# A transformer stack in fp32 on one core: the opening in one stage, norm first and bias tables last

## The chip, the core and the metric

The kernel runs on one core of one Trainium2 chip. The metric is the device time of one execution in microseconds (us), as the median of several runs. The engines are named as the profile names them: PE is the matrix engine (TensorE), PEld its weight load, DVE is VectorE, ACT is ScalarE, POOL is GpSimd, SP is SyncE. SP and ACT also issue transfers (DMAs), each on a queue of its own: the profile calls SP's queue q1 and ACT's q10. Both feed the same 16 DMA engines.

## The reference, cut to what matters

The program computes a whole stack: first a dilated attention layer and a state space layer, then four layers of other kinds, each with a feed forward part. Sequence 512, width 1024, all in fp32. The change touches only what comes ahead of the first projections, and three tables of relative position bias that later layers read.

```python
h = rms_norm(x, attn_pre_norm[0])                 # x: (1, 512, 1024)
proj = h @ w_in                                   # w_in: 1024 x 10240
for g, (window, dilation) in enumerate(((128, 1), (512, 4), (2048, 16))):
    bias = rel_bias[t5_bucket(jnp.maximum(back, 0) * dilation)]      # table bias_a
    logits = einsum(q, k) * scale + bias
...
# layers 0 and 3 of the second part read a causal 512-wide table (bias_d),
# layer 2 a windowed 256-wide one (bias_s), both from rel_bias of that part
s = jnp.where(rel >= 0, s + bias, -jnp.inf)
```

## The kernel before, in words

**Weights.** All weights are one stream of 270 chunks of 128x2048 fp32 (1 MB each). SP loads chunk c into one of two `raw` buffers; POOL splits it into a high part `wh` and a low part `wl` (two instructions, two buffers of each); PE multiplies both with the split activations `XTh` and `XTl`, three matmuls for one product (`three`, lines 326 to 328). Three rules tie the stream together. `load_chunk` (line 290) issues the load of chunk c once chunk c-2 has been split (`w_split`). `split_chunk` (lines 296 and 298) begins on chunk c once it has landed and once PE has used chunk c-2 (`w_used`). PE waits for the split of chunk c at its first tile. Chunks are counted from 0.

**The opening.** It has two stages, each a block that all engines enter and leave together.
- `setup` (line 370 on): SP loads chunks 0 to 3 and POOL splits chunks 0 and 1. ACT issues the loads of two one-hot matrices (33 rows), of the small bias tables, of x and of four norm vectors. PE makes the three tables by four matmuls of one-hot by bias (line 436), DVE copies them out of PSUM to `ta` (16 heads x 893) and `tb` (16 x 1022). ACT then issues five transfers that write each row of a table 128 times to HBM, each time shifted by one element (`toeplitz`, line 423): three for `bias_a` (rows of 256, 128 and 128 elements), one for `bias_d` (16 heads x 128 rows x 512), one for `bias_s` (16 x 128 x 256). The profile's 2048 KB, 1024 KB and so on of line 423 are the sizes of these; together 10 MB. Then ACT leaves the block.
- `norm_phase("pre")`: ACT takes the squares of X (line 501), POOL turns the sums into factors (480, 481), DVE scales X by rows into `N` (546), PE transposes N (587), DVE multiplies by the norm weight, a column now (532), ACT copies the high part (515), DVE forms the low part (535). SP waits for `bias_a` to be in HBM before the block ends.

**The attention stage** (`dilated_attention`, one block). It uses chunks 0 to 39 in four passes of ten. Ahead of the passes PE makes the 18 tiles of chunks 0 to 5 without a break (four v tiles for chunk 0, two for chunk 1, four for 2, two for 3, four for 4, two for 5), through two PSUM banks that ACT empties in turn (`take`, lines 1338 to 1344). In the passes such tiles are filled in between the steps of eight attention jobs. ACT loads a pair of heads of `bias_a` to `B` (line 1387), first ahead of its first `take`, then once a half pass. SP runs the stream for chunks 4 on (`sp_stream`) and waits for all tables before it leaves the block.

```python
        def toeplitz(dst, table, off, w, sig=bias_a_stored):
            x = table[:, off:off + w]
            src = bass.AP(x.tensor, x.offset + P - 1, [list(x.ap[0]), [-1, P], [1, w]])
            act.dma_start(dst, src).then_inc(sig.h, 16)
```

Of the kernel before, what the change touches and what calls it, by code (L numbers as in the profile page):

```python
# [23 lines left out]
P = 128  # L24
S = 512
D = 1024
# [191 lines left out]
def build(nc, t, out):  # L218

    ctx = ExitStack()  # L220
    with ctx:
# [70 lines left out]
        def split_chunk(pool, c, r, s):  # L292
# [4 lines left out]
            pool.wait_ge(w_high.h, c + 1)  # L297
            pool.tensor_tensor(wl[s][:, :], raw[r][:, :], wh[s][:, :].bitcast(F32), ALU.subtract).then_inc(w_split.h, 1)  # L298

        def stream(eng, first, last, unit, one):  # L300
# [57 lines left out]
        x_back = signal("x_back")  # L358
        v_moved = signal("v_moved")
        bias_ds_stored = signal("bias_ds_stored")  # L360

        def wait_bias_stored(eng):
# [7 lines left out]
        def setup(a_scope, b_scope):  # L370

            with ExitStack() as c:
                tb = sb("tb", [HEADS, LB], F32, b_scope)
                ta = sb("ta", [HEADS, LA], F32, a_scope)
# [3 lines left out]
                made = signal("made")  # L378
                tables = signal("tables")
                with nc.Block() as block:  # L380
                    @block.sync
                    def _(sp):
                        for k in range(min(RAW, NCH)):
                            sp.dma_start(raw[k][:, :], t["weights"][k]).then_inc(raw_in[k].h, 16)
                        for k in range(RAW, min(RAW + SPLIT, NCH)):
                            load_chunk(sp, k, k % RAW)

                    @block.gpsimd
                    def _(pool):
                        link = InOrder(pool, pool_order)  # L390
                        link(pool.memset(zero[:, :], 0.0))
# [7 lines left out]
                        link.done()  # L399
                        for s in credited:  # L400
                            pool.sem_inc(s.h, CREDIT)
                        for k in range(min(SPLIT, NCH)):
                            pool.wait_ge(raw_in[k % RAW].h, 16 * (k // RAW + 1))
                            pool.tensor_tensor(wh[k][:, :], raw[k % RAW][:, :], zero[:, :].to_broadcast([P, CHUNK]), ALU.add).then_inc(w_high.h, 1)
                            pool.wait_ge(w_high.h, k + 1)
                            pool.tensor_tensor(wl[k][:, :], raw[k % RAW][:, :], wh[k][:, :].bitcast(F32), ALU.subtract).then_inc(w_split.h, 1)

                    @block.scalar
                    def _(act):
                        for d, s in ((oh_a[:, :], t["onehot_a"]), (oh_b[:, :], t["onehot_b"]),  # L410
                                     (rb[0:32, 0:HEADS], t["rel_bias"]), (rb[0:32, HEADS:], t["rel_bias_2"]),
                                     (X[:, :, :], t["x"].rearrange("b (t p) d -> p (b t) d", p=P)),
                                     (col[:, 0:KT], t["attn_pre_norm"]), (col[:, KT:2 * KT], t["ssm_pre_norm"]),
                                     (col[:, 16:18], t["da_subln_2"]), (col[:, 18:19], t["hg_gnorm_2"])):
                            act.dma_start(d, s).then_inc(loaded.h, 16)

                        act.wait_ge(tables.h, 4)

                        def toeplitz(dst, table, off, w, sig=bias_a_stored):

                            x = table[:, off:off + w]
                            src = bass.AP(x.tensor, x.offset + P - 1, [list(x.ap[0]), [-1, P], [1, w]])
                            act.dma_start(dst, src).then_inc(sig.h, 16)
                        toeplitz(bias_a[:, :, 0:W1], ta, 0, W1)
                        toeplitz(bias_a[:, :, W1:384], ta, L1, W2)
                        toeplitz(bias_a[:, :, 384:512], ta, L1 + L2, W2)
                        toeplitz(bias_d, tb, 0, WD, bias_ds_stored)
                        toeplitz(bias_s, tb, LD_, WS, bias_ds_stored)
                        act.wait_ge(loaded.h, 16 * 9)

                    @block.tensor
                    def _(pe):
                        pe.wait_ge(loaded.h, 16 * 9)
                        pe.wait_ge(made.h, 2)
                        for n, (o, lo, hi, r) in enumerate(((oh_a, 0, 512, 0), (oh_a, 512, LA, 0), (oh_b, 0, 512, 1), (oh_b, 512, LB, 1))):
                            nc.tensor.matmul(PS[n][0:HEADS, 0:hi - lo], rb[:, HEADS * r:HEADS * r + HEADS], o[:, lo:hi],
                                             start=True, stop=True).then_inc(p_b.h, 1)

                    @block.vector
                    def _(dve):  # L440
                        for n, (o, lo, hi) in enumerate(((ta, 0, 512), (ta, 512, LA), (tb, 0, 512), (tb, 512, LB))):
                            dve.wait_ge(p_b.h, n + 1)
                            nc.vector.tensor_copy(o[:, lo:hi], PS[n][0:HEADS, 0:hi - lo]).then_inc(tables.h, 1)
                loaded.base += 16 * 9
                p_b.base += 4

# [795 lines left out]

        sink_tmp = sb("sink_tmp", [P, 8])

        def dilated_attention():
            c0 = pos[0]
            with ExitStack() as c:
                O3 = sb("O3", [P, 3, 8, S], F32, c)  # L1250
# [2 lines left out]
                with ExitStack() as c2:  # L1253
# [98 lines left out]
                    with nc.Block() as block:  # L1352
                        @block.sync
                        def _(sp):
                            sp_stream(sp, 40)
                            wait_bias_stored(sp)

                        @block.gpsimd
                        def _(pool):
                            pool_stream(pool, 40)  # L1360

                        @block.tensor
                        def _(pe):
# [11 lines left out]
                                    att[half].pe(at, fill)  # L1375
                            for n in range(len(first)):
                                project(pe, 0, 0, 0, n)
                            with pe.Fori(0, PASSES - 1) as i:
                                one_pass(i, False)
                            one_pass(PASSES - 1, True)  # L1380
# [2 lines left out]
                        def _(act):  # L1383
# [5 lines left out]
                            def one_pass(i, last):  # L1389
                                for half in range(2):  # L1390
# [32 lines left out]
                        @block.vector  # L1423
                        def _(dve):
                            link = InOrder(dve, dve_order)
                            with dve.Fori(0, PASSES) as i:
                                link.enter(i, sum(x.dve_links() for x in att))
                                for half in range(2):
# [16 lines left out]
                    PROJ.base += 4 * n_proj  # L1445
                    BIAS_IN.base += 128
                    BIAS_USED.base += 8
                    pos[0] += 40
                combine_groups(O3, MX, SM)

# [1122 lines left out]


        with ExitStack() as b_scope:
            with ExitStack() as a_scope:
                setup(a_scope, b_scope)
                if "attn" in STAGES:
                    norm_phase("pre", gain=col[:, 0:KT], before_end=wait_bias_a_stored)
                else:  # L2580
                    norm_phase("plain", before_end=wait_bias_stored)
            if "attn" in STAGES:
                dilated_attention()
        if "attn" in STAGES:
            out_phase(None, (t["attn_post_norm"][0],), False)
        if "ssm" in STAGES:
# [61 lines left out]
```

## Time and profile before

| What | us |
|---|---|
| median of 3 runs | 4982.3 (4978.52 to 4989.15) |
| the profiled execution | 4992.26 |
| its span in the trace | 4990.5 |
| busy in the span: PE, PEld, DVE, POOL, ACT | 4028.2, 3288.4, 2437.1, 2381.6, 930.3 |
| granted clock of PE, mean of the span | 0.873 of full |

The profile is one execution. Its page gives the busy time of each engine and the costliest groups of instructions; the trace behind it gives instructions in order of time, transfers with their time from issue to landing, and the work of any stretch. The span is 1.8 us shorter than the execution that it comes from, and that execution is 10 us above the median.

### The profile page before, as it was taken

How to read it: one execution, taken by the hardware profiler on the slowest of the kernel's cores; microseconds unless marked ns; L12 is line 12 of the kernel's file. 1: busy time of each engine (PE TensorE's matmuls, PEld its weight loads, DVE VectorE, ACT ScalarE, POOL GpSimd, SP SyncE). 2: the span in 40 equal slices, each digit the busy share in tenths (PEclk: the TensorE clock that was granted, in tenths of full speed). 3: DMA queues.
4: the chain of work that ended last, by engine and by line, in shares of the span. 5: the costliest groups of instructions: out<-in, count | busy, mean ns of one | idle time of the engine just before them, and what ended most of it. 6: DMA issues, size and time to landing. Idle time of an engine off the chain costs nothing. (4 is left out here: it accounts for less than half of the span.)

```text
span 4990.5 us, 51634 instructions
## 1 busy us (share of the span) xinstructions
PE 4028.2 (81%) x18540; PEld 3288.4 (66%) x18540; DVE 2437.1 (49%) x3019; ACT 930.3 (19%) x2251; POOL 2381.6 (48%) x687
## 2 busy tenths in 40 slices
PE   2999999745467875998895579987789988758997
PEld 1887887434455654887685568866568866646886
DVE  1223224478434564564336645544555535655563
ACT  0133233110021221110103311112510112221110
POOL 1534433133005433677474347764147755316774
PEclk9999999677558977999997689998789999868998
DMA  8211111123622111222120012221122222102221
GB/s 128 72 68 64 55 67 56 42 67 115 118 67 81 68 59 42 85 99 94 68 93 26 0 68 93 93 79 64 38 72 97 92 80 77 64 30 85 93 96 68
DMA packets 105245, 364.97 MB, mean 73 GB/s; under 512 B 24631, under 2 KB 51511, under 8 KB 69513
## 3 DMA queue, kind: packets, MB, share of 16 engines
q1 hardware_dynamic: 72528, 321.49, 18.9%
q10 hardware_dynamic: 32568, 41.44, 3.8%
q8 instruction: 102, 1.67, 0.1%
q14 instruction: 47, 0.38, 0.0%
HBM read 336.75 MB, written 30.34 MB: 74 GB/s over the span
## 5 line engine op out<-in xcount | busy, mean ns | idle before, releaser
L296 POOL TENSOR_TENSOR wh<-raw,zero 128x2048 fp32r<-128x2048 f32 x268 | 983.4, 3669 | 2189.8 <-PE bank L328 2189.8
L298 POOL TENSOR_TENSOR wl<-raw,wh 128x2048 fp32r<-128x2048 f32 x268 | 1257.7, 4693 | 21.0
L326 PE MATMUL bank<-XTh,wh 128*128 128x512 f32 x2128 | 850.1, 399 | 62.6 <-DVE XTl L2559 39.9
L327 PE MATMUL bank<-XTh,wl 128*128 128x512 f32 x2128 | 838.4, 394 | 0.0
L328 PE MATMUL bank<-XTl,wh 128*128 128x512 f32 x2128 | 837.6, 394 | 0.0
L326 PE MATMUL bank<-wh,XTh 128*128 128x512 f32 (+2 forms) x1440 | 536.8, 373 | 66.1 <-PEq L468 32.4
L327 PE MATMUL bank<-wh,XTl 128*128 128x512 f32 (+2 forms) x1440 | 530.5, 368 | 0.0
L328 PE MATMUL bank<-wl,XTh 128*128 128x512 f32 (+2 forms) x1440 | 529.6, 368 | 0.0
L326 PEld LDWEIGHTS bank<-XTh,wh 128*128 128x128 f32 x2128 | 406.3, 191 | 172.6 <-issue 86.9
L328 PEld LDWEIGHTS bank<-XTl,wh 128*128 128x128 f32 x2128 | 405.3, 190 | 86.8
L327 PEld LDWEIGHTS bank<-XTh,wl 128*128 128x128 f32 x2128 | 406.5, 191 | 82.1
L326 PE MATMUL bank<-wh,HTh 128*128 128x512 f32 x1024 | 404.5, 395 | 0.0
L327 PE MATMUL bank<-wh,HTl 128*128 128x512 f32 x1024 | 404.5, 395 | 0.0
L328 PE MATMUL bank<-wl,HTh 128*128 128x512 f32 x1024 | 404.4, 395 | 0.0
L326 PEld LDWEIGHTS bank<-wh,XTh 128*128 128x128 f32 x1440 | 318.3, 221 | 117.5 <-issue 82.8
L756 DVE TENSOR_TENSOR Q<-R 128x512 f32<-128x512 f32 x128 | 317.1, 2477 | 109.8 <-ACT R L742 108.7
L758 DVE TENSOR_TENSOR HTl<-Q,HTh 128x512 fp32r<-128x512 f32 x128 | 320.8, 2506 | 89.5 <-ACT HTh L744 89.5
L327 PEld LDWEIGHTS bank<-wh,XTl 128*128 128x128 f32 x1440 | 318.6, 221 | 31.6
L328 PEld LDWEIGHTS bank<-wl,XTh 128*128 128x128 f32 x1440 | 317.7, 221 | 31.7
L1179 DVE TENSOR_TENSOR SC<-bank,B 128x256 f32<-128x256 f32 (+2 forms) x128 | 66.9, 523 | 491.0 <-PE bank L1147 489.0
L766 DVE TENSOR_TENSOR Y<-Y,bank 128x512 f32<-128x512 f32 x128 | 88.0, 688 | 402.7 <-PE bank L328 402.7
L587 PE MATMUL bank<-ident,X 128*128 128x128 f32 x384 | 82.2, 389 | 198.0 <-DVE X L559 141.6
(313 smaller groups left out, 5089.9 us busy)
## 6 DMA issues: line engine op xcount, KB each, us to landing
raw<-in_weights SPq DMA_DIRECT2D x270, 1024.0 KB, 4.8
MO<-ssm_out SPq DMA_DIRECT2D x8, 1024.0 KB, 4.8
B<-bias_d ACTq DMA_DIRECT2D x8, 1024.0 KB, 5.5
bias_d<-tb ACTq DMA_DIRECT2D x1, 4096.0 KB, 63.1
B<-bias_a ACTq DMA_DIRECT2D x8, 512.0 KB, 5.8
ssm_out<-CA SPq DMA_DIRECT2D x16, 256.0 KB, 2.6
ssm_in<-W2T SPq DMA_DIRECT2D x8, 512.0 KB, 2.7
ssm_out<-lag_kernel SPq DMA_DIRECT2D x16, 256.0 KB, 4.8
```

The costliest lines, as they stand in the source:

```text
L296: pool.tensor_tensor(wh[s][:, :], raw[r][:, :], zero[:, :].to_broadcast([P, CHUNK]), ALU.add).then_inc(w_high.h, 1)
L298: pool.tensor_tensor(wl[s][:, :], raw[r][:, :], wh[s][:, :].bitcast(F32), ALU.subtract).then_inc(w_split.h, 1)
L326: nc.tensor.matmul(psum, sh, mh, start=first, stop=False)
L327: nc.tensor.matmul(psum, sl, mh, start=False, stop=False)
L328: return nc.tensor.matmul(psum, sh, ml, start=False, stop=last)
L587: r = nc.tensor.transpose(PS[n % 4][:, P * k:P * k + P], src[:, tt, 512 * half + P * k:512 * half + P * k + P], ident[:, :])
L756: v.tensor_tensor(Q[u % 2][:, :], R[u % 2][:, :], R[u % 2][:, :], ALU.mult).then_inc(sq_done.h, 1)
L758: v.tensor_tensor(HTl[:, u, :], Q[u % 2][:, :], HTh[:, u, :].bitcast(F32), ALU.subtract).then_inc(low_done.h, 1)
L766: v.tensor_tensor(y, y, PS[4 + tt][:, :], ALU.add).then_inc(down_free.h, 1)
L1179: r = v.tensor_tensor(o, s, b.unsqueeze(1).to_broadcast([P, m, w]), ALU.add)
```

## The change

The two stages of the opening become one, `begin`, and the writing of the tables moves into the attention stage.

- SP loads X in four parts ahead of chunks 0 and 1 and no other chunk; the norm weight comes to `gain` as a row repeated over all partitions.
- ACT takes the squares of each part of X as it lands. DVE makes N = X * factor * gain in one instruction (line 484). PE transposes to banks 0, 1, 6, 7, ACT copies the high part straight from PSUM, and DVE subtracts it straight from PSUM. POOL splits chunk 0 only; the split of chunk 1 opens the attention stage.
- The four table matmuls come after the transposes, into banks 2 to 5. DVE copies them out at the start of the attention stage. `ta` now lies in the end of Y, which is free until pass 4.
- SP, not ACT, issues the tables, among the loads of the chunks. `bias_d` and `bias_s` are each cut into four transfers of four heads. ACT waits for all of `bias_a` ahead of its fifth `take`.

```diff
         def wait_bias_stored(eng):
             wait_bias_a_stored(eng)
-            eng.wait_ge(bias_ds_stored.h, 16 * 2)
+            eng.wait_ge(bias_ds_stored.h, 16 * 2 * 4)
...
-                        for k in range(min(RAW, NCH)):
+                        for tt in range(TT):
+                            sp.dma_start(X[:, tt, :], xt[:, tt, :]).then_inc(x_in[tt].h, 16)
+                        for k in range(2):
                             sp.dma_start(raw[k][:, :], t["weights"][k]).then_inc(raw_in[k].h, 16)
-                        for k in range(RAW, min(RAW + SPLIT, NCH)):
-                            load_chunk(sp, k, k % RAW)
...
+                        def square(tt):
+                            act.wait_ge(x_in[tt].h, 16)
+                            nc.scalar.activation(N[:, tt, :], X[:, tt, :], ACT.Square, scale=D ** -0.5,
+                                                 accum_out=st[:, tt:tt + 1]).then_inc(squared.h, 1)
...
+                        for tt in range(TT):
+                            dve.wait_ge(g_b.h, g_b.base + tt + 1)
+                            v.scalar_tensor_tensor(N[:, tt, :], X[:, tt, :], st[:, tt:tt + 1], gain[:, :], ALU.mult, ALU.mult).then_inc(scaled.h, 1)
+                            if tt:
+                                halves(tt - 1)
+                        halves(TT - 1)
...
                         def _(sp):
-                            sp_stream(sp, 40)
+                            ta = Y[:, :, :].rearrange("p a b -> p (a b)")[0:HEADS, 3 * D:3 * D + LA]
+                            load_chunk(sp, 2, 0)
+                            sp.wait_ge(tables.h, 4)
+                            toeplitz(sp, bias_a[:, :, 0:W1], ta, 0, W1, bias_a_stored)
+                            load_chunk(sp, 3, 1)
+                            toeplitz(sp, bias_a[:, :, W1:384], ta, L1, W2, bias_a_stored)
+                            toeplitz(sp, bias_a[:, :, 384:512], ta, L1 + L2, W2, bias_a_stored)
+                            at = SPLIT + RAW
+                            for k in range(4):
+                                stream(sp, at + 4 * k, at + 4 * k + 4, RAW, lambda c, k: load_chunk(sp, c, k % RAW))
+                                heads = slice(4 * k, 4 * k + 4)
+                                toeplitz(sp, bias_d[heads], tb[heads], 0, WD, bias_ds_stored)
+                                toeplitz(sp, bias_s[heads], tb[heads], LD_, WS, bias_ds_stored)
+                            stream(sp, at + 16, at + 40, RAW, lambda c, k: load_chunk(sp, c, k % RAW))
                             wait_bias_stored(sp)

                         @block.gpsimd
                         def _(pool):
+                            split_high(pool, 1)
+                            split_low(pool, 1)
                             pool_stream(pool, 40)
...
-                            load_bias(0, 0, 0)
                             for n in range(len(first)):
+                                if n == TT:
+                                    wait_bias_a_stored(act)
+                                    load_bias(0, 0, 0)
                                 take(act, 0, 0, 0, n)
...
-            with ExitStack() as a_scope:
-                setup(a_scope, b_scope)
-                if "attn" in STAGES:
-                    norm_phase("pre", gain=col[:, 0:KT], before_end=wait_bias_a_stored)
...
+            begin(tb)
+            dilated_attention(tb)
```

**SP's queue, before.** From the first chunk load to the stream of the attention stage; the tables are on ACT's queue.

```order
L384 DMA raw0<-in_weights 128x2048
L384 DMA raw1<-in_weights 128x2048
L290 DMA raw0<-in_weights 128x2048 [waits w_split]
L290 DMA raw1<-in_weights 128x2048 [waits w_split]
L380 UNCONDITIONAL_BRANCH
L470 UNCONDITIONAL_BRANCH [waits barrier_Pool_Activation_PE_DVE_SP_release]
L468 UNCONDITIONAL_BRANCH [waits bias_a_stored]
L1353 UNCONDITIONAL_BRANCH [waits barrier_Pool_Activation_PE_DVE_SP_release]
```

In the changed kernel the same queue reads so, from the end of `begin` on; the lines 290 are chunks 2 and 3, then a loop over chunks 4 to 7, and the first part of the tables of `tb` stands behind chunk 7.

```order
L1405 UNCONDITIONAL_BRANCH [waits barrier_Pool_Activation_PE_DVE_SP_release]
L290 DMA raw0<-in_weights 128x2048 [waits w_split]
L497 DMA bias_a<-Y 2048x1x256 [waits tables]
L290 DMA raw1<-in_weights 128x2048 [waits w_split]
L497 DMA bias_a<-Y 2048x1x128 x2
L315 UNCONDITIONAL_BRANCH
L315 ISA
L290 ISA [waits w_split]
L290 DMA raw0<-in_weights 128x2048
L290 ISA [waits w_split]
L290 DMA raw1<-in_weights 128x2048
L315 REGISTER_ALU
L315 COMPARE_AND_BRANCH
L497 DMA bias_d<-tb 512x1x512
L497 DMA bias_s<-tb 512x1x256
L315 UNCONDITIONAL_BRANCH
```

The table transfers now stand between the loads on the queue of the weights: `bias_a` around chunk 3, and 512 rows (four heads by 128) of `bias_d` and of `bias_s` ahead of chunks 8, 12, 16 and 20.

**ACT, before**, at the start of the attention stage: the bias pair is loaded ahead of the first tile that ACT takes out of PSUM.

```order
L1382 UNCONDITIONAL_BRANCH [waits barrier_Pool_Activation_PE_DVE_SP_release]
L1387 DMA B<-bias_a 128x2x512
L1343 ACTIVATE V<-bank 128x128 [waits proj_done]
L1344 ACTIVATE X<-bank 128x128
L1343 ACTIVATE V<-bank 128x128 [waits proj_done]
```

And ACT in the changed kernel, from the tile before the load on:

```order
L1395 ACTIVATE V<-bank 128x128 [waits w_used]
L1396 ACTIVATE X<-bank 128x128
L1455 DMA B<-bias_a 128x2x512 [waits bias_a_stored]
L1390 ACTIVATE QK<-bank 128x512 [waits proj_done]
L1390 ACTIVATE QK<-bank 128x512 [waits w_used]
```

The load, and with it a wait for the whole of `bias_a`, has moved from before the first tile to between the fourth (the last of chunk 0) and the fifth; the block that came before no longer holds that wait.

## Rows read from the trace of the kernel before

**Rows 1.** Stretches, us: busy by engine (instructions), PE clock, DMA share, GB/s.
```profile
22.80:84.50 61.70, 0.00 (x0) 0.00 (x0) 0.00 (x0) 0.00 (x0) 0.03 (x1) 1.00 0.80 107
...
107.80:138.00 30.20, 27.48 (x150) 25.45 (x151) 0.00 (x0) 2.88 (x10) 9.18 (x3) 0.87 0.86 116
138.00:600.00 462.00, 453.68 (x2171) 393.59 (x2171) 128.48 (x225) 123.45 (x375) 207.31 (x52) 0.98 0.18 64
```

**Rows 2.** The opening in order of time: start, length, engine, line, operation.
```profile
4.78 0.55 ACTq L415 DMA_DIRECT2D col<-in_hg_gnorm  x1
...
15.47 3.15 PE L436 MATMUL bank<-oh_a,rb 33*16 33x512 f32 x4 [15.47 <-DMA col<-in_hg_gnorm]
...
22.07 0.68 DVE L443 COPY tb<-bank 16x510 f32<-16x510 f32 x1 [1.02 <-PE bank L436]
22.78 28.79 ACTq L423 DMA_DIRECT2D bias_a<-ta  x3
...
84.51 1.28 ACT L501 ACT_TABLE_LOAD   x1 [84.51 <-PEq L380]
85.81 1.06 ACT L501 ACTIVATE N<-X 128x1024 f32<-128x1024 f32 x1
...
90.79 0.63 ACT L515 ACTIVATE XTh<-tmp 128x512 fp32r<-128x512 f32 x1 [0.72 <-DVE tmp L532]
...
106.70 0.69 DVE L535 TENSOR_TENSOR XTl<-tmp,XTh 128x512 fp32r<-128x512 f32 x1 [0.70 <-ACT XTh L515]
107.69 10.31 ACTq L1387 DMA_DIRECT2D B<-bias_a  x1
...
107.86 0.55 PE L326 MATMUL bank<-wh,XTh 128*128 128x256 f32 x1 [6.40 <-PEq L468]
```

**Rows 3.** DVE in the whole span: the operation that N = X * factor * gain uses.
```profile
L559 DVE SCALAR_TENSOR_TENSOR X<-Y,st,bc 128x1024 f32<-128x1024 f32 x32 | 41.1, 1285 | 8.8 <-POOL st L481 8.0
```

**Rows 4.** Line 423, the table transfers: issues, and time from issue to landing.
```profile
L423 ACTq DMA_DIRECT2D bias_a<-ta x3: 720/7957/20045, 22.8 to 31.5; - x3
...
DMA to landing us min/median/max: 25.2/40.2/74.2
```

**Rows 5.** POOL in order of time: the splits of chunks 2, 3 and 5.
```profile
126.22 3.60 POOL L296 TENSOR_TENSOR wh<-raw,zero 128x2048 fp32r<-128x2048 f32 x1 [34.48 <-PE bank L328]
129.90 4.61 POOL L298 TENSOR_TENSOR wl<-raw,wh 128x2048 fp32r<-128x2048 f32 x1
137.03 3.60 POOL L296 TENSOR_TENSOR wh<-raw,zero 128x2048 fp32r<-128x2048 f32 x1 [2.52 <-PE bank L328]
...
170.25 3.60 POOL L296 TENSOR_TENSOR wh<-raw,zero 128x2048 fp32r<-128x2048 f32 x1 [2.55 <-PE bank L328]
```

**Rows 6.** Columns as in rows 1: only `bias_d`, then only `bias_s` being written.
```profile
75.00:110.00 35.00, 9.12 (x42) 8.08 (x43) 13.16 (x20) 10.59 (x17) 4.01 (x8) 0.79 0.90 98
116.00:130.00 14.00, 11.46 (x67) 10.74 (x68) 0.00 (x0) 1.68 (x8) 3.70 (x2) 0.88 0.82 95
```

**Rows 7.** The transfers of the first 10 us: packets by size and by queue.
```profile
DMA packets 623, 2.97 MB, mean 297 GB/s; under 512 B 151, under 2 KB 151, under 8 KB 367
...
q1 hardware_dynamic: 288, 2.10, 57.3%
...
q14 instruction: 1, 0.00, 0.0%
```

**Rows 8.** Line 1387, the load of a bias pair: time from issue to landing, 8 issues.
```profile
DMA to landing us min/median/max: 3.5/5.8/31.1
```

**Rows 9.** The page's transfers: chunk loads, KB each and us to landing.
```profile
raw<-in_weights SPq DMA_DIRECT2D x270, 1024.0 KB, 4.8
```

**Rows 10.** PE in order of time: the first matmul on chunks 8, 16 and 20.
```profile
243.64 0.50 PE L326 MATMUL bank<-XTh,wh 128*128 128x512 f32 x1
...
395.67 0.79 PE L326 MATMUL bank<-XTh,wh 128*128 128x512 f32 x1
...
466.96 0.39 PE L326 MATMUL bank<-wh,XTh 128*128 128x256 f32 x1
```

More of the change, by code:

```diff
@@ L360, in build, with begin @@
         bias_ds_stored = signal("bias_ds_stored")
+        tables = signal("tables")
         def wait_bias_stored(eng):
             wait_bias_a_stored(eng)
[L365 removed]
+            eng.wait_ge(bias_ds_stored.h, 16 * 2 * 4)
         def wait_bias_a_stored(eng):
             eng.wait_ge(bias_a_stored.h, 16 * 3)
[L370 removed]
+        def begin(tb):
             with ExitStack() as c:
[L373 to L374 removed]
                 oh_a = sb("oh_a", [33, LA], F32, c)
@@ L377, in setup @@
                 rb = sb("rb", [33, 2 * HEADS], F32, c)
-                made = signal("made")
-                tables = signal("tables")
+                N = sb("N", [P, TT, D], F32, c)
+                gain = sb("gain", [P, D], F32, c)
+                made, oh_in = signal("made"), signal("onehots_in")
+                x_in = [signal(f"x_in{tt}") for tt in range(TT)]
+                squared, scaled, turned, gain_in = signal("squared"), signal("scaled"), signal("turned"), signal("gain_in")
+                high, low = signal("x_high"), signal("x_low")
+                HOLD = (0, 1, 6, 7)
+                xt = t["x"].rearrange("b (t p) d -> p (b t) d", p=P)
                 with nc.Block() as block:
@@ L398, in _, with rsqrt @@
                         pool.wait_ge(made.h, 2)
-                        link.done()
                         for s in credited:
                             pool.sem_inc(s.h, CREDIT)
[L402 to L406, printed above, removed]
+                        def rsqrt(tt):
+                            pool.wait_ge(squared.h, tt + 1)
+                            r = st[:, tt:tt + 1]
+                            link(pool.tensor_scalar(r, r, 1.0, RMS_EPS, ALU.mult, ALU.add))
+                            pool.tensor_tensor(r, r, mhalf[:, :], ALU.pow).then_inc(g_b.h, 1)
@@ L408, in _ @@
+                        for tt in range(TT):
+                            rsqrt(tt)
+                        split_high(pool, 0)
+                        split_low(pool, 0)
+                        link.done()
                     @block.scalar
                     def _(act):
[L410 to L426, printed above, removed]
@@ L427, in _ @@
-                        toeplitz(bias_d, tb, 0, WD, bias_ds_stored)
-                        toeplitz(bias_s, tb, LD_, WS, bias_ds_stored)
-                        act.wait_ge(loaded.h, 16 * 9)
+                        for d, s, sig in ((gain[:, :], t["attn_pre_norm"][0].partition_broadcast(P), gain_in),
+                                          (oh_a[:, :], t["onehot_a"], oh_in), (rb[0:32, 0:HEADS], t["rel_bias"], oh_in),
+                                          (rb[0:32, HEADS:], t["rel_bias_2"], oh_in), (oh_b[:, :], t["onehot_b"], oh_in),
+                                          (col[:, KT:2 * KT], t["ssm_pre_norm"], loaded),
+                                          (col[:, 16:18], t["da_subln_2"], loaded), (col[:, 18:19], t["hg_gnorm_2"], loaded)):
+                            act.dma_start(d, s).then_inc(sig.h, 16)
@@ new lines, in square, with copy_high @@
+                        def square(tt):
+                            act.wait_ge(x_in[tt].h, 16)
+                            nc.scalar.activation(N[:, tt, :], X[:, tt, :], ACT.Square, scale=D ** -0.5,
+                                                 accum_out=st[:, tt:tt + 1]).then_inc(squared.h, 1)
+                        def copy_high(n):
+                            tt, half = n // 2, n % 2
+                            act.wait_ge(turned.h, n + 1)
+                            nc.scalar.activation(XTh[:, 4 * half:4 * half + 4, P * tt:P * tt + P],
+                                                 PS[HOLD[n % 4]][:, :].rearrange("p (k c) -> p k c", k=4), ACT.Copy).then_inc(high.h, 1)
@@ L431, in _ @@
+                        for tt in range(TT):
+                            square(tt)
+                        for n in range(2 * TT):
+                            copy_high(n)
                     @block.tensor
                     def _(pe):
-                        pe.wait_ge(loaded.h, 16 * 9)
                         pe.wait_ge(made.h, 2)
+                        for n in range(2 * TT):
+                            tt, half = n // 2, n % 2
+                            pe.wait_ge(scaled.h, tt + 1)
+                            if n >= 4:
+                                pe.wait_ge(low.h, n - 3)
+                            for k in range(4):
+                                r = nc.tensor.transpose(PS[HOLD[n % 4]][:, P * k:P * k + P],
+                                                        N[:, tt, 512 * half + P * k:512 * half + P * k + P], ident[:, :])
+                            r.then_inc(turned.h, 1)
@@ L440, in _, with halves, toeplitz @@
                     def _(dve):
[L441 to L445, printed above, removed]
+                        v = nc.vector
+                        link = InOrder(dve, dve_order)
+                        def halves(tt):
+                            for n in (2 * tt, 2 * tt + 1):
+                                half = n % 2
+                                dve.wait_ge(high.h, n + 1)
+                                xs = (slice(None), slice(4 * half, 4 * half + 4), slice(P * tt, P * tt + P))
+                                v.tensor_tensor(XTl[xs], PS[HOLD[n % 4]][:, :].rearrange("p (k c) -> p k c", k=4), XTh[xs].bitcast(F32),
+                                                ALU.subtract).then_inc(low.h, 1)
+                        dve.wait_ge(gain_in.h, 16)
+                        for tt in range(TT):
+                            dve.wait_ge(g_b.h, g_b.base + tt + 1)
[3 more added lines that the diff above has]
+                        halves(TT - 1)
+                        dve.wait_ge(loaded.h, 16 * 3)
+                        link.done()
+                loaded.base += 16 * 3
+                g_b.base += TT
+        def toeplitz(eng, dst, table, off, w, sig):
+            x = table[:, off:off + w]
+            src = bass.AP(x.tensor, x.offset + P - 1, [list(x.ap[0]), [-1, P], [1, w]])
+            eng.dma_start(dst, src).then_inc(sig.h, 16)
         BN = [st[:, 16 + 12 * tt:28 + 12 * tt] for tt in range(TT)]
@@ L1377, in _ @@
                                 project(pe, 0, 0, 0, n)
+                            pe.wait_ge(tables.h, 4)
                             with pe.Fori(0, PASSES - 1) as i:
@@ L1425, in _ @@
                             link = InOrder(dve, dve_order)
+                            ta = Y[:, :, :].rearrange("p a b -> p (a b)")[0:HEADS, 3 * D:3 * D + LA]
+                            for n, (o, lo, hi) in enumerate(((ta, 0, 512), (ta, 512, LA), (tb, 0, 512), (tb, 512, LB))):
+                                dve.wait_ge(p_b.h, p_b.base + n + 1)
+                                nc.vector.tensor_copy(o[:, lo:hi], PS[2 + n][0:HEADS, 0:hi - lo]).then_inc(tables.h, 1)
                             with dve.Fori(0, PASSES) as i:
```

20 lines of the change are left out of this document (13 added, 7 removed).

## The prediction

> **What bounds the kernel now.** I read the busy times by stretch first. From 22.8 to 84.5 us no engine computes, yet the DMA engines are 0.80 busy; from 138 to 600 PE is busy for 453.7 of 462 us at a clock of 0.98 of full, with DMA at 0.18 [rows 1]. So the opening is bound by transfers and the attention stage by PE. The order of time says which transfers: ACT starts to issue tables at 22.8, and only at 84.5 does it get to the norm, because issuing them held it [rows 2]. PE's first projection starts at 107.9 [rows 2]. What the change can win lies ahead of that; what it can lose lies in the attention stage, where a late chunk stops a PE that has no idle time to give.
>
> **Step 1, the new opening.** The wait for the tables goes. ACT issues its eight loads until about 5.3 (eight as before; the last began at 4.78 [rows 2]), loads its function table (1.28) and takes four squares of 1.06: 10.9. X comes first on SP's queue and is there in parts by then. DVE's four scalings cost 1.29 each [rows 3], ACT's high parts 0.63 and DVE's low parts 0.69 [rows 2], now without the extra pass by the norm weight. DVE's chain of about 2.7 a quarter, after a start near 10, ends near 20.5. PE's transposes end near 19; behind them stand the four table matmuls, which took 6.6 (15.47 to DVE's last copy at 22.07 [rows 2]), so PE ends the block at about 25.6. Chunk 0 is split by then. With the 0.4 us that such a boundary takes, and starting up, the first projection comes at 26.5, **81 us earlier**.
>
> **Step 2, the gate at the fifth tile.** DVE copies the tables at the start of the stage (four copies of at most 0.68): SP issues `bias_a` at about 29. Before, `bias_a` took from 22.8 to 71.7 (the last of its three was issued at 31.5; I take the median of 40.2 as its time to landing [rows 4]): 48.9 us, one chunk load among them. Now chunk 3 is that load, and the tail of chunk 2's adds 1: all landed at 79. Until then ACT stands ahead of its fifth take, and the takes of two more tiles stand behind it; PE makes chunks 0 and 1 by about 49 and stops. It starts on chunk 2 at 80, where it did at 137.0 [rows 5]: 57 earlier. It starts with the low clock: in the stretch with the first projections the mean clock was 0.87 [rows 1], which over 30 us is 4 us of full clock, idle time included; I take 2 of it. **Lead 55.** So the tables still decide 26 us of the opening, in another place.
>
> **Step 3, the first part of the other tables.** PE has used chunk 3 at 170.2 [rows 5] less 55 = 115.2. POOL splits chunk 5 (3.60 + 4.61 and gaps = 8.3 [rows 5]): 123.5. SP issues chunk 7's load and behind it 1.0 MB of `bias_d` and 0.5 MB of `bias_s`. A chunk load takes 4.8 us [rows 9], of which I put 4.1 on the way before the part begins and 3.3 after it for chunk 8 (its rows still have to move, and land).
>
> How long is such a part? Before, the whole tables moved at 98 and 95 GB/s [rows 6], over 16 DMA engines: 6.1 and 5.9 GB/s for each. If a part of four heads is spread over 16 engines too, it takes 1.57 MB / 97 = 16.3 us. If it is spread over four, it takes 1.049 / 24.5 + 0.524 / 23.8 MB per GB/s = 42.8 + 22.1 = 65. The rows that tell are of the first 10 us [rows 7]. Two chunks landed: 288 packets, 2 x 128 rows and 2 x 16 small closing ones. Of 151 packets under 512 B, 32 are those, 1 is for instructions, 64 are rows of the two small bias tables; 54 are left to close four transfers. The two small tables have 32 rows, the one-hots 33. With 16 each it would be 64; 54 is 16 + 16 + 11 + 11. So a transfer of 33 rows ran on 11 engines, the largest number up to 16 that divides 33, and a source of four heads should run on 4. I take 65, and 1.5 more for bias pairs and instructions that use the same four engines: **66.4**.
>
> The Trainium skill, "DMA: Bandwidth & Descriptors", section "Why a DMA increments its semaphore by 16 and not by 1", states the same as a rule: the largest number up to 16 that divides the slowest dimension of both sides. By it the part is 4 engines wide. The Trainium skill, on the same page (section "Specifications"), gives about 27 GiB/s for one engine, by which four engines would need, as an estimate, 13.6 us for a part and nothing would be lost; the trace disagrees, with 6.1 GB/s for an engine on this source.
>
> Does chunk 8 wait for the part? The bias pair issued at 107.7 on the queue of the tables landed 31.1 us later, where others took 5.8 [rows 8] at the median: a transfer waits for what stands ahead of it on its queue. On four engines that will be the part. So: 123.5 + 4.1 + 66.4 + 3.3 = 197.3 for chunk 8, split by 205.6. PE began on chunk 8 at 243.6 [rows 10]: **the lead is down to 38**.
>
> **Step 4, three more parts.** From chunk 8's arrival the next part follows by POOL and SP alone: two splits (16.6), chunk 11's load ahead (4.1), the part (66.4), chunk 12 (3.3): a round of 90.4. PE had 152.0 us from chunk 8 to 16 and 71.3 from 16 to 20 [rows 10], 223.3 for three rounds; now they take 271.2. PE starts on chunk 20 at 205.6 + 271.2 = 476.8 instead of 467.0, and pays 2 for the low clock after the last stop: **12 us behind**. The stalls are about 17, 24, 5 to 10 and 17 to 20. After chunk 20 no part is left, and neither the later chunks nor the later layers change.
>
> Costed at nothing: the chunk loads behind `bias_a` (hidden by PE's stop), the split of chunk 1 on POOL (8.3 us under chunk 0's tiles), SP's end of block wait (hundreds of us after the last part), the norm row. If the stop in step 2 were gone, chunk 4 behind `bias_a` would be late instead.
>
> **The number.** The sum is -81.4 + 24.4 + 2 + 67 = +12 on the profiled execution (4992.3), which is 10 above the median. On the median: 4982.3 + 12 = **4994.3**. About 0.2% (10 us) is what a measurement of this kernel can tell from no change, so this is slower by little more than that. One us on a part is 4 us in the end: parts of 61.5 to 71.5 us give -8 to +32, 4974 to 5014.
>
> **The rivals.**
> 1. *Parts of no consequence* (0.15): a part runs on all 16 engines at 97 GB/s, or finds a faster way from few. At 16.3 us chunk 8 lands by 147 and is split in time; nothing stalls up to a part of about 48. Then the lead of step 2 stays: 4982.3 - 55 = 4927, faster. For it: no transfer of this kernel has a source of four partitions, so nothing shows one slow. Against it: the 54 closing packets, and 6.1 GB/s for an engine.
> 2. *Parts half as bad* (0.13): four engines share less among themselves than 16 did (if what held the tables to 98 GB/s was at their source or target), and each moves 6.5 to 8 GB/s: parts of 48 to 61 us, -55 to -10; I put 4960 for it. For it: rows of 2 KB and of 1 KB ran at 98 and 95 GB/s [rows 6], nearly alike, as under one shared limit; against it: each head still has one engine to itself, before and after.
> 3. *Parts worse* (0.17): the queue fills. Issuing the first tables held ACT for 28.8 us and B's for 10.3 [rows 2], so SP may be held likewise, and ACT's bias pairs may have to wait behind SP's rows; DVE waits for a pair at each half pass. With 7 us more in each round: 4994 + 28 = 5022.
> 4. *The change does not do what it says*: were the start of the projections not earlier, the 55 us of step 2 would be missing, 5049. The order of the queues speaks against it: no table stands ahead of the first projection any more. I give it no chance of its own.
>
> **How the numbers follow.** The forecast has 0.55: 0.25 within 0.2%, 0.30 slower. Rival 1 gives 0.15 faster, rival 2 0.10 faster and 0.03 same, rival 3 0.17 slower. Faster 0.25, same 0.28, slower 0.47. The range runs from 4927, rival 1, to 5022, rival 3; half of each lies outside.
>
> **What would show it.** Step 1: first projection at 26 to 28 us. Step 2: PE idle from about 49 to 80, ACT's wait put down to `bias_a`. Step 3: DMA share near 0.25 and some 24 GB/s on top of the weights while a part runs, `bias_d` parts landing about 45 us after issue, `bias_s` parts about 65. Step 4: POOL waiting for `raw` four times, PE idle ahead of chunks 8, 12, 16 and 20, about 65 us in all, and none ahead of others. Parts that land in under 20 us, or PE without stops after 80 us, would prove it wrong; so would a stop at a half pass that ends with a landed bias pair.

## The result and the profile after

| | before | changed |
|---|---|---|
| median of 8 runs, us | 4982.6 (4975.3 to 4989.2) | 5005.3 (4995.4 to 5018.9) |
| ratio, 95% interval | | 1.0043 (1.003 to 1.0056) |
| profiled execution, its span | 4992.3, 4990.5 | 5007.2, 5005.3 |
| first projection starts | 107.9 | 33.5 |
| PE's first matmul on chunk 2, 8, 16, 20 | 137.0, 243.6, 395.7, 467.0 | 85.6, 206.5, 382.4, 469.1 |

The kernel became slower by 0.43%, 23 us by the medians and 15 us by the two profiled executions. It starts its projections 74 us earlier, and has lost all of that at chunk 20.

The opening in order of time, with the columns of [rows 2]:

```profile
14.35 3.60 POOL L303 TENSOR_TENSOR wh<-raw,zero 128x2048 fp32r<-128x2048 f32 x1 [0.54 <-DMA raw<-in_weights]
14.62 4.41 DVE L484 SCALAR_TENSOR_TENSOR N<-X,st,gain 128x1024 f32<-128x1024 f32 x1
18.03 5.38 POOL L308 TENSOR_TENSOR wl<-raw,wh 128x2048 fp32r<-128x2048 f32 x1
18.96 1.28 DVE L479 TENSOR_TENSOR XTl<-bank,XTh 128x512 fp32r<-128x512 f32 x2
...
20.16 4.33 DVE L484 SCALAR_TENSOR_TENSOR N<-X,st,gain 128x1024 f32<-128x1024 f32 x1
...
26.44 3.15 PE L466 MATMUL bank<-oh_a,rb 33*16 33x512 f32 x4
```

No table stands in front of the norm any more. The last two scalings took 4.4 and 4.3 us, though, where the same operation took 1.285 [rows 3], while POOL was splitting chunk 0; so the table matmuls start at 26.4 and the stage at 33.

PE, the waits for longest in total from 80 to 520 us (waiting engine and line, what it waited for, us in total, times, longest):

```profile
PE bank L336 <- POOL wl L298: 32.7, 4, 15.3
PE bank L336 <- ACT QK L1390: 27.2, 1, 27.2
PE bank L1206 <- DVE SC L1253: 10.7, 3, 8.6
PE bank L1199 <- issue: 4.1, 1, 4.1
```

The 27.2 us are the gate at the fifth tile. The 32.7 us in four are the late chunks: 15.3 ahead of chunk 8, 4.5 ahead of 12, 0.7 ahead of 16 and 12.2 ahead of 20. Of the 10.7, the stop of 8.6 ended behind a late bias pair: DVE stood for the pair until 256, and PE for DVE until 260. It came before the stop ahead of chunk 12:

```profile
256.07 0.75 DVE L1231 TENSOR_TENSOR SC<-bank,B 128x128 f32<-128x128 f32 x2 [20.86 <-DMA B<-bias_a]
...
293.74 0.59 PE L336 MATMUL bank<-wh,XTh 128*128 128x256 f32 x1 [4.54 <-POOL wl L298]
```

POOL, the splits of chunks 8, 12 and 20 (that of 16 began at 374.09), columns as in [rows 5]:

```profile
198.16 3.60 POOL L296 TENSOR_TENSOR wh<-raw,zero 128x2048 fp32r<-128x2048 f32 x1 [37.38 <-DMA raw<-in_weights]
...
285.44 3.60 POOL L296 TENSOR_TENSOR wh<-raw,zero 128x2048 fp32r<-128x2048 f32 x1 [36.86 <-DMA raw<-in_weights]
...
460.84 3.60 POOL L296 TENSOR_TENSOR wh<-raw,zero 128x2048 fp32r<-128x2048 f32 x1 [33.83 <-DMA raw<-in_weights]
```

POOL stood 31 to 37 us ahead of each of the four, for the load behind a part of the tables: 138.7 us in all. The rounds between them are 87.3, 88.7 and 86.8 us. The transfers from 130 to 172 us, GB/s in 40 slices of 1.05 us:

```profile
GB/s 429 359 68 25 25 23 23 25 25 25 25 23 23 25 25 23 25 25 23 23 25 25 23 41 25 23 25 25 23 27 23 23 25 25 23 33 25 23 23 25
```

And a stretch inside it, columns as in [rows 1]:

```profile
140.00:149.00 9.00, 9.00 (x41) 7.67 (x41) 0.00 (x0) 1.04 (x3) 7.24 (x2) 1.00 0.23 25
```

Chunk 7 goes through, all but its end, in the first two slices at 360 to 430 GB/s; then the part runs, nearly alone, at 25 GB/s, where rows of the same table ran at 98 before [rows 6], and the 16 DMA engines are 0.23 busy: as many as four of them.

### The profile page after: what moved, and what is told of

Same layout as the page of the kernel before. It is cut to its first block and busy times, and to the rows that moved or that the text cites. A ratio compares the mean times of both kernels' runs of the same rounds, so it can differ in the third digit from the quotient of the medians.

```text
span 5005.3 us, 51620 instructions
## 1 busy us (share of the span) xinstructions
PE 4051.9 (81%) x18540; PEld 3308.8 (66%) x18540; DVE 2434.6 (49%) x3011; ACT 930.1 (19%) x2251; POOL 2380.0 (48%) x687
## 5 line engine op out<-in xcount | busy, mean ns | idle before, releaser
L336 PE MATMUL bank<-wh,XTh 128*128 128x512 f32 (+2 forms) x1440 | 539.9, 375 | 101.5 <-ACT QK L1390 27.2
```

The costliest lines, as they stand in the source:

```text
L336: nc.tensor.matmul(psum, sh, mh, start=first, stop=False)
```

## The experiments

Two questions were open. Does a part of the tables take 65 us because four DMA engines move it, or because four heads lie side by side? And are the gate and the opening worth what the waits say? All runs are edits of the changed kernel unless said. The times of the kernel before that stand beside them were taken on the same chip: 4986.8 for e1 to e4, 4989.5 for e5 to e8.

### e1_rows16: rows instead of heads

```diff
-                                toeplitz(sp, bias_d[heads], tb[heads], 0, WD, bias_ds_stored)
-                                toeplitz(sp, bias_s[heads], tb[heads], LD_, WS, bias_ds_stored)
+                                toeplitz(sp, bias_d[:, 32 * k:32 * k + 32, :], tb, 0, WD, bias_ds_stored, 32 * k, 32)
+                                toeplitz(sp, bias_s[:, 32 * k:32 * k + 32, :], tb, LD_, WS, bias_ds_stored, 32 * k, 32)
```

The last two arguments are the first row and the number of rows.

> Each part of bias_d and bias_s is 32 rows of all 16 heads instead of 128 rows of 4 heads: the same 1.5 MB in the same place of SP's queue, but 16 heads in the slowest dimension. Theory (a part is as slow as one engine's share of its heads): 16 engines at 6.1 GB/s, a part in 16 to 17 us, no stop of PE ahead of chunks 8, 12, 16 and 20; chunk 20 starts at about 417 us instead of 469 in the changed kernel, and the median falls by about 50, to 4955. Rival (the bytes or the place in the queue cost, not the width): parts stay near 65 us or still stop PE by some 10 us each, and the time stays within 10 of 5005.

Measured: 4945.7 (4942.9 to 4957.9), 0.9933 of before (0.9914 to 0.9952). Of PE's waits in the same stretch the late chunks and the bias pair are gone and the gate is left, and POOL waits for no load. The second row is at the end of the first pass, where the kernel before has 1.9:

```profile
PE bank L336 <- ACT QK L1390: 27.3, 1, 27.3
PE bank L1199 <- issue: 4.6, 1, 4.6
```

The same bytes in the same place of the queue cost nothing that shows when they move at 96 GB/s. What the parts cost the changed kernel is all in their shape: some 60 us by the medians, 64 by the two profiled spans (5005.3 and 4940.9), 55 by the two ratios. Of the 64, 55 are there at chunk 28; the rest comes behind it, where the two kernels are the same. It does not yet tell width from neighbourhood: 16 heads are both 16 engines and four groups of neighbours.

### e4_strided: four heads, not side by side

```diff
-                                heads = slice(4 * k, 4 * k + 4)
+                                heads = slice(k, HEADS, 4)
```

> The changed kernel, but part k holds heads k, k+4, k+8 and k+12 instead of heads 4k to 4k+3: still four heads, so by width still four engines, but their rows lie in four places of SBUF that are four partitions apart. Theory (each engine moves 6.1 GB/s from such a source by itself): a part stays at 65 us and the median at 5005. Rival (engines that read neighbouring partitions share one way out of SBUF, about 25 GB/s for a group of four partitions): each engine gets up to four times as much, a part takes under 20 us, PE has no stops, and the median is near 4955.

Measured: 4946.9 (4937.7 to 4948.2), 0.9923 (0.9905 to 0.994): my theory fell, the rival holds. The views of stretches inside `bias_d`'s first part, columns as in [rows 1]; here e4_strided:

```profile
136.00:146.00 10.00, 10.00 (x45) 9.26 (x45) 0.00 (x0) 0.89 (x4) 3.89 (x2) 1.00 0.26 101
```

and here e1_rows16:

```profile
136.00:146.00 10.00, 10.00 (x45) 9.22 (x45) 0.00 (x0) 0.89 (x4) 4.11 (x2) 1.00 0.83 96
```

DMA share 0.26 of 16 engines is four, and they move 101 GB/s, 25 each. Sixteen engines move 96, and are 0.83 busy for it. So an engine alone is not limited to 6 GB/s; in the changed kernel it was waiting for something that it shared with others. What the two fast runs have in common is that their heads lie in four groups of four partitions.

The Trainium skill, "SBUF — State Buffer", section "Door 1: The DMA port swizzle (why `[64,N]` ≈ `[32,N]`)", says that transfers reach SBUF through 16 ports, and that partitions 0 to 3 are on one of them, 4 to 7 on another, and so on to 31. Its table gives 27.6 GB/s as measured on partitions 0 to 3 and 104 on partitions 0 to 15. The trace agrees: 25 GB/s from heads 0 to 3, 98 from all 16 heads [rows 6].

### e5_stride2: two groups

```diff
-                                heads = slice(4 * k, 4 * k + 4)
+                                heads = slice(8 * (k // 2) + k % 2, 8 * (k // 2) + 8, 2)
```

> The changed kernel, but a part holds every second head (0, 2, 4, 6; then 1, 3, 5, 7; then 8, 10, 12, 14; then 9, 11, 13, 15): four engines as before, heads in two groups of four neighbouring partitions instead of one (changed kernel, 25 GB/s) or four (the run with every fourth head, 100 GB/s). Theory (a group of four neighbouring partitions gives 25 GB/s in all): 50 GB/s, a part in 31 to 33 us, under the 48 us from which chunk 8 is late, so no stops: median as in the run with every fourth head, near 4947. Rival (only heads in four different groups are fast, the rest is slow as before): 25 GB/s, median near 5005.

Measured: 4948.1 (4942.4 to 4954.3), 0.9916 (0.9894 to 0.9938). A stretch inside the first part:

```profile
137.00:155.00 18.00, 17.23 (x81) 14.58 (x81) 0.65 (x2) 1.64 (x4) 10.73 (x3) 1.00 0.25 51
```

Again four engines, now 51 GB/s. One group gives 25, two give 51, four give 101: the rate goes with the groups of neighbouring partitions, at the same number of engines.

One rival is left by these edits: they also change how far apart the four heads are written in HBM. The traces have it. In `bias_d` neighbouring heads are 256 KB apart, in `bias_s` 128 KB. So e5_stride2's `bias_s` is written at the distance of the changed kernel's `bias_d`, 256 KB, and e4_strided's `bias_s` at that of e5_stride2's `bias_d`, 512 KB. The stretches inside `bias_s`, e5_stride2 first, then e4_strided:

```profile
158.50:161.50 3.00, 2.12 (x10) 1.42 (x8) 2.93 (x4) 0.68 (x3) 2.25 (x1) 1.00 0.23 50
...
144.00:147.50 3.50, 3.50 (x17) 2.92 (x16) 0.00 (x0) 0.13 (x1) 3.42 (x2) 1.00 0.27 97
```

At 256 KB it is 25 GB/s from one group and 50 from two; at 512 KB it is 51 from two and 97 from four. The distance in HBM does not set the rate, the groups at the source do.

And twice the time of e4_strided's parts costs nothing, as the time in hand said: POOL waits for no load in either, and PE starts on chunk 20 at 417.6 here and 417.2 there.

### e2_gate_late: the gate moved

```diff
                             for n in range(len(first)):
-                                if n == TT:
-                                    wait_bias_a_stored(act)
-                                    load_bias(0, 0, 0)
                                 take(act, 0, 0, 0, n)
+                            wait_bias_a_stored(act)
+                            load_bias(0, 0, 0)
```

> The changed kernel, with ACT's wait for bias_a and the first load of a pair moved behind all 18 takes of chunks 0 to 5. Theory: PE's stop from 58 to 85.5 us goes; it runs on to chunk 4, whose load stands behind bias_a (landed near 88, split near 96), so chunk 5 is split some 23 us earlier, the first part of four heads starts that much earlier, and as the parts pace the stage all later starts move by 23: median about 4982. Rival (the parts are late whatever PE does): chunk 8 still lands at 198, and the time stays within 5 of 5005.

Measured: 4976.0 (4969.1 to 4985.4), 0.9981 of before (0.997 to 0.9992), 29 less than the changed kernel and more than the 23 of the theory. SP issues the first part at 104.4 instead of 128.3, PE starts on chunk 20 at 445.8 instead of 469.1, 23 us earlier as the theory had it. The parts still pace the stage, with POOL waiting 139.1 us for four loads. Up to chunk 40 the lead over the changed kernel stays near 23; what is above it comes behind, where the two kernels are the same.

### e3_split_late: the scalings undisturbed

```diff
+                        pool.wait_ge(scaled.h, TT)
                         split_high(pool, 0)
                         split_low(pool, 0)
```

> The changed kernel, but POOL begins to split chunk 0 only when DVE has scaled all four quarters of X. Theory (POOL's split slowed DVE's scalings from 1.28 to 4.4 us): all four take 1.28 us, the last transposes and the table matmuls end 6 us earlier, the first projection starts at 27 instead of 33.4, the median falls by about 6, to 4999. Rival (the 4.4 us come from something else, such as the landing of X or the low clock of another engine): they stay at 4.4 us, and the later split of chunk 0 costs up to 6 us more.

Measured: 4994.6 (4983.3 to 5001.4), 1.0017 (1.0005 to 1.0028), 11 less than the changed kernel. DVE in order of time:

```profile
14.64 1.28 DVE L485 SCALAR_TENSOR_TENSOR N<-X,st,gain 128x1024 f32<-128x1024 f32 x1
...
17.03 1.28 DVE L485 SCALAR_TENSOR_TENSOR N<-X,st,gain 128x1024 f32<-128x1024 f32 x1
```

The first projection starts at 27.3 instead of 33.5: the 6.2 us were POOL's split. At chunk 28 the run is 8 us ahead of the changed kernel; what comes behind that is within the wander between executions. DVE's scaling reads X and the norm row, both in SBUF. The subtraction beside it, which has one operand in PSUM, took 1.28 for two in both kernels, with POOL at work (the row at 18.96 above) or without. The Trainium skill, "SBUF — State Buffer", section "🔬 SBUF: two separate sides", has it as a lock: a DVE operation with two SBUF inputs and a GpSimd operation that reads SBUF exclude each other. The rows agree: POOL's first half ran from 14.35 to 17.95, and the scaling that began at 14.62 ended at 19.03, 1.08 after it, a little less than its own 1.28; POOL's second half, which began at 18.03, took 5.38, 0.88 more than the 4.50 that it takes in this run, where DVE's scalings are over.

The trace of the kernel before has such a case too, in the attention stage: a DVE operation on two SBUF operands, while POOL split chunk 10 (259.0 to 267.3). The five of its form ahead of it took 0.69 each.

```profile
263.26 4.54 DVE L1201 TENSOR_TENSOR SC<-SC,stats 128x512 f32<-128x512 f32 x1
```

### e6_best, e8_best2: the edits together

e6_best is e1_rows16 with the edits of e2_gate_late and e3_split_late.

> Three edits together: parts by 32 rows of all 16 heads, ACT's wait for bias_a behind the 18 takes, chunk 0 split after the scalings. Theory: the gains add, since no part paces the stage any more: 4946 less 22 (PE starts on chunk 4 at 90 instead of 118) less 6 (opening): near 4918. Rival (without the stop at the fifth tile the weights behind bias_a are late, and the parts of the tables start so early that they meet chunks with less time in hand): it keeps 10 to 20 of these 28 us only, 4928 to 4936.

Measured: 4924.2 (4914.1 to 4928.0), 0.9865 (0.9843 to 0.9886), 65 us less than before. That is 6 from the sum and 4 from the rival's best; what is missing shows in PE's waits from 27 to 420 us, where the longest is:

```profile
PE bank L336 <- POOL wl L298: 5.7, 1, 5.7
```

The 5.7 us are ahead of chunk 4, whose load stands behind all of `bias_a`. The next, of 5.5, is at the end of the first pass, where e1_rows16 has 4.6. Hence e8_best2, where SP issues that load ahead of the last piece of `bias_a`:

```diff
                             toeplitz(sp, bias_a[:, :, W1:384], ta, L1, W2, bias_a_stored)
+                            load_chunk(sp, 4, 0)
                             toeplitz(sp, bias_a[:, :, 384:512], ta, L1 + L2, W2, bias_a_stored)
...
-                                stream(sp, at + 4 * k, at + 4 * k + 4, RAW, lambda c, k: load_chunk(sp, c, k % RAW))
+                                stream(sp, at + 4 * k + (k == 0), at + 4 * k + 4, RAW, lambda c, k: load_chunk(sp, c, k % RAW))
```

> The run with the three edits, and chunk 4's load put ahead of the last piece of bias_a. Theory: chunk 4 no longer lands behind all of bias_a (about 82 instead of there near 83 to 88) and is split by the time PE has used chunk 3, so PE's short stop ahead of chunk 4 (3.5 us with the late gate alone) goes: 3 us less than without this edit. Rival (POOL's split of chunk 4 waits for PE to use chunk 2, not for the load): no difference.

Measured: 4918.6 (4912.9 to 4931.9), 0.9869 (0.9845 to 0.9892). The two intervals lie on each other, so the times do not tell these two apart. The trace does: the stop of 5.7 us is gone (the wait is no longer among PE's), and the steps after it start 5.5 us earlier (chunk 20 at 387.0 instead of 392.5).

### e7_before: the kernel before, once more

> The kernel before, unchanged, for a second profile. Theory (the 10 us by which the changed kernel falls behind after chunk 20 are 5 us at the end of the second pass, which all changed kernels have, and otherwise wander between executions): the end of the second pass shows PE idle for 1.9 us without a named releaser again, and the later chunks shift against the first profile by some us up and down. Rival (a real cost of the change after chunk 20): the two profiles of the kernel before agree within 2 us everywhere.

One profile, 4986.7 us. PE's waits from 560 to 620 us, here, at the end of the second pass,

```profile
PE bank L1147 <- issue: 2.0, 1, 2.0
```

and in the changed kernel:

```profile
PE bank L1199 <- issue: 5.1, 1, 5.1
```

The first profile of before has 1.9 there; the changed kernel and its seven variants have 4.7 to 5.3. The end of the first pass is alike: 1.8 and 1.9 in the two of before, 3.8 to 5.5 in the others. I aligned the profiles chunk by chunk by POOL's splits. The two of before drift from 5.5 us one way (chunk 67) to 5.7 the other (chunk 228) and end 5.6 apart, so the rival, which had them agree within 2, fell. A few us at the end of a span say nothing by themselves; a step within one pass that several kernels share does.

The changed kernel stands at +2.2 against the first profile when PE starts on chunk 20, at +5.3 for chunk 27 and at +10.4 for chunk 28 (the end of the second pass). Then it wanders up to +18.8 and back to +14.9 for the last chunk. Of the 12.7 us behind chunk 20, some 3 come right behind the last stop, where the granted clock was 0.71 from 469 to 480 and 1.00 in the kernel before from 467 to 480. The next 5 come in one step, in a place where no transfer of a table is left; PE's wait there is 3.2 longer than before, and no releaser shows. The same step is in all changed kernels (4.8 to 6.1) and is 1.1 in the second profile of before. The last 4.5 are within what two executions of one kernel differ by. What makes the step I did not test: the loop's code lies elsewhere in each kernel, and I have no run that moves code alone.

## Why the prediction was right, and where it was not

**What came as forecast.** Slower, 5005.3 in the range of 4927 to 5022; the likeliest value, 4994.3, is 11 too low. The chain came as forecast too: the gate, four parts on four engines, rounds set by POOL and SP. By the profiled executions it was +12 against +15, but that is closer than the working deserves: chunk 20 came 2.1 behind where the sum had 12 with its low clock, and 12.7 came behind chunk 20 where the sum had nothing.

**Step 1.** First projection at 26.5 forecast, 33.5 measured; the gain was 74 and not 81. The error is DVE's chain of 2.7 us a quarter: I took the scaling's 1.29 from a place where POOL was not splitting. e3_split_late shows that this is 6.2 of the 7; its opening ends at 27.3. The row at 263.26 of the kernel before could have warned me.

**Step 2.** `bias_a` took 48.6 us (35.7 to 84.3) against 48.9, and PE stood from 58 to 85.6. The lead at chunk 2 was 51.4 instead of 57, and 51.0 at chunk 3: step 1's miss, carried on. Of the 2 us for the low clock only 0.5 were there: chunk 2 took 22.9 us (85.6 to 108.5) against 22.4 before (137.0 to 159.4). e2_gate_late confirms that the gate cost 23 us at chunk 20.

**Step 3.** The time was right, the mechanism was half wrong. Chunk 8 landed at 198.2 (197.3 forecast), lead 37 (38), and two errors cancel in it: the part began 4 us late and was 3 us shorter. The part does run on four engines, as the count of closing packets gave: DMA share 0.23 and 25 GB/s. But "6.1 GB/s for each engine" was wrong as a property of an engine. e4_strided moves 25 GB/s on each of four engines from the same kind of rows. The product came out right by luck: 98 / 16 x 4, four engines of sixteen, and 98 / 4, one group of four, are the same number. For the same reason I was wrong that the trace speaks against the figure for one engine; it spoke of a limit at the source that the engines share. What could have warned me: all source rows of the tables lie in 16 neighbouring partitions.

**Step 4.** Rounds of 87.3, 88.7 and 86.8 us against 90.4: the part was some 3 us shorter than 66.4. Its 1.57 MB at 25 GB/s make 63, so both the 65 and my 1.5 us for other traffic were too much. PE started on chunk 20 at 469.1 against 476.8, 2.1 us behind before and not 10. The stops were misjudged: I forecast about 65 us of them ahead of the four chunks, and they were 32.7 (15.3, 4.5, 0.7 and 12.2). The sum does not rest on them: the arrival of the chunk behind each part sets the pace, whatever PE does in between. From chunk 3 to chunk 20 the lead fell by 53 us, where the sum had 65 from chunk 2; the 12 less are 3 for each of the four parts. Of the 53, the waits for DVE (the bias pair above all) and at the end of the first pass are 12 more than before, and the other 9 are PE taking longer over its work. Behind the stops its granted clock was 0.5 of full, the lower of its two levels, for some us (206 to 212, 260 to 266, 294 to 296, 468 to 474); I had 2 us for that. How much of the 9 the clock makes I did not separate.

Rival 3's stop was there too: the bias pairs landed up to 21 us after issue (median 19.2) where 5.8 is usual [rows 8], DVE waited 42.4 us for two of them, and PE stood 8.6 us behind the first. By the prediction's own list, a stop at a half pass that ends with a landed bias pair spoke against it. As far as the chunks show, the stop lay inside the time that the next part set anyway: the rounds are no longer than their sum. SP was held 6.8 to 15.7 us over the second issue of each part, as rival 3 had it, without effect on the rounds.

**After chunk 20.** "After chunk 20 no part is left, and neither the later chunks nor the later layers change" failed by 5 us at the end of the second pass, a term that the sum had at nothing; its cause stays open. With the 3 us behind the last stop and the wander, it brought the profiled difference from +2 back to +15, near the forecast. The medians differ by 23; the other 8 are between a profile of before that was 10 above its median and one of after that was 2 above its own.

**The rivals.** What I gave 0.15, no loss from the parts, is what the same bytes do with one number in a slice changed: 4945.7 to 4948.1, and its "finds a faster way from few" was right about what few engines can do. Rival 2 named the true kind of limit, one shared at the source, and drew the wrong way from it: four heads side by side share less among themselves only if they lie in several groups, and these lie in one.

## What to carry to other kernels

A transfer moved onto the queue of the weights costs nothing as long as it is shorter than the time in hand between a load's issue and its use, and everything beyond that once in each round. Here the estimate for that time was 48 us; parts of 31 us fitted, parts of 63 did not, and nothing between was tried. When a transfer is cut into parts, cut it so that every part still reads all the groups of partitions that the whole did. A cut into four blocks of neighbouring partitions cut the rate by four here and cost some 60 us; the same cut with every fourth partition in a part cost nothing. And measure a rate with its sharers: a rate per engine taken from a trace may belong to whatever the engines queue for, until a second shape says otherwise.

## What the runs showed of the hardware that I had not expected

- Four DMA engines moved 101 GB/s out of SBUF from four partitions that are four apart, 51 from two groups of two, and 25 from four side by side, with rows of 2 KB; with rows of 1 KB it was 97, 50 and 23.
- A DVE operation of 1.28 us on two SBUF operands took 4.3 to 4.4 while POOL split weights, and POOL's subtraction 5.38 instead of 4.5; the DVE subtraction with an operand in PSUM was not slowed (1.28 for two).
- A 512 KB load on ACT's queue landed in 17.9 to 21.0 us, where 5.8 is usual, the three times that it was issued beside a part on SP's queue, although only four engines had that part, and in 7.2 with no part beside it. So a queue of its own does not keep a load clear of a slow part. What made it wait, the engines or their source, was not tested: in e4_strided no such load was issued beside a part.
